# A hybrid diffusion backbone: DeltaNet on unnormalized keys and queries, with state and outputs beside the inverse

## The reference

```python
q = l2_normalize(heads(q)); k = l2_normalize(heads(k))      # x * rsqrt(sum(x*x) + 1e-6)
q = q * dk ** -0.5
kb = k * beta[..., None]
m = where(strict, (kb @ k^T) * decay, 0)
t_inv = inverse(eye + m)
u = t_inv @ (v * beta[..., None])
w = t_inv @ (kb * exp(gam)[..., None])
qk = (q @ k^T) * decay
for each chunk:                       # s is the state, carried on
    v_new = u - w @ s
    o = (q * exp(gam)[..., None]) @ s + qk @ v_new
    s = s * exp(g_last) + (k * exp(g_last - gam)[..., None])^T @ v_new
o = rms_norm(o, norm_w) * silu(z)     # norm per head over 128, eps 1e-6
```

## Time and profile before

| | |
|---|---|
| median of three executions | 2689.41 us |
| the profiled execution | 2687.36 us, span 2685.6 us, mean granted clock 0.967 |
| busy | PE 2487.0 (93%), DVE 1599.0 (60%), ACT 1000.0 (37%), POOL 80.3 (3%) |
| chain that ended last | PE 84%, DVE 9%, ACT 3%, issue 2% |
| costliest group | L1314, u products: 3 x 2208 matmuls, 811.4 + 799.8 + 799.1 us |
| 30 reciprocals of DVE, L1793 | 92.5 us, 3082 ns each |
| DeltaNet's matmuls of 64 columns, L1612 | x3952, 234.4 us |

### The profile page before, as it was taken

One profiled execution on the slowest core, in us unless ns is written; L12 is line 12 of the kernel. 1 busy time (PEld: TensorE's weight loads), 2 busy tenths in 40 slices (PEclk: granted clock), 3 DMA queues, 4 the chain that ended last, 5 costly groups with the idle time before them and its releaser, 6 DMA issues.

```text
span 2685.6 us, 37159 instructions
## 1 busy us (share of the span) xinstructions
PE 2487.0 (93%) x15516; PEld 2068.9 (77%) x15516; DVE 1599.0 (60%) x2342; ACT 1000.0 (37%) x1551; POOL 80.3 (3%) x108
## 2 busy tenths in 40 slices
PE   3999998989888999989999989999898968899999
PEld 1888876857678778868887868888685758889899
DVE  5777665367766674577655553333446676566654
ACT  2322223355653422233222232232246563344543
POOL 0000000000012100000000000000000002200000
PEclk8999999999889999999999999999999989999999
DMA  6455542101100043325554422222220210045454
GB/s 256 173 188 188 188 157 94 63 32 63 63 32 2 17 157 110 125 96 204 187 190 169 157 88 94 100 104 95 94 95 32 94 63 2 2 144 186 158 185 161
DMA packets 44661, 309.62 MB, mean 115 GB/s; under 512 B 5072, under 2 KB 6224, under 8 KB 7632
## 3 DMA queue, kind: packets, MB, share of 16 engines
q1 hardware_dynamic: 44208, 305.98, 31.6%
q10 hardware_dynamic: 288, 1.27, 0.1%
HBM read 306.18 MB, written 1.05 MB: 114 GB/s over the span
## 4 chain that ended last, share of the span: by engine, by line
PE 84%; DVE 9%; ACT 3%; issue 2%; DMA 1%; SPq 0%; ACTq 0%; DVEq 0%
PE bank L1314 69%; PE bank L1612 7%; PE bank L1307 2%; DVE rt L1793 2%; PE bank L1558 1%; PE bank L1536 1%; DVE w_lo L1782 1%; DMA ring<-in_wts 1%; DVE u_lo L1822 1%; DVE sq L1832 1%; ACT L850 1%; PE bank L1545 1%; ACT w_hi L832 1%; PE bank L1345 1%; DVE work L2184 1%
## 5 line engine op out<-in xcount | busy, mean ns | idle before, releaser
L1782 DVE TENSOR_TENSOR w_lo<-ring,w_hi 128x1024 fp32r<-128x1024 f32 x420 | 510.8, 1224 | 704.9 <-ACT w_hi L832 700.9
L1314 PE MATMUL bank<-u_hi,w_hi 128*128 128x512 f32 (+1 forms) x2208 | 811.4, 367 | 85.6 <-DVE w_lo L1782 48.6
L1314 PE MATMUL bank<-u_hi,w_lo 128*128 128x512 f32 (+1 forms) x2208 | 799.8, 362 | 0.0
L1314 PE MATMUL bank<-u_lo,w_hi 128*128 128x512 f32 (+1 forms) x2208 | 799.1, 362 | 0.0
L832 ACT ACTIVATE w_hi<-ring 128x1024 fp32r<-128x1024 f32 x420 | 443.0, 1058 | 884.0 <-PE bank L1314 882.2
L1314 PEld LDWEIGHTS bank<-u_hi,w_hi 128*128 128x128 f32 x2208 | 422.8, 191 | 166.3 <-issue 67.3
L1314 PEld LDWEIGHTS bank<-u_hi,w_lo 128*128 128x128 f32 x2208 | 423.2, 192 | 65.0 <-issue 3.1
L1314 PEld LDWEIGHTS bank<-u_lo,w_hi 128*128 128x128 f32 x2208 | 422.4, 191 | 63.6
L1612 PE MATMUL bank<-work 64*64 64x64 f32 (+1 forms) x3952 | 234.4, 247 | 37.9 <-DVE work L2187 21.4
L1612 PEld LDWEIGHTS bank<-work 64*64 64x64 f32 (+1 forms) x3952 | 221.8, 161 | 50.0 <-POOL work L806 31.8
L1314 PE MATMUL bank<-hidden_hi,w_hi 128*128 128x512 f32 (+1 forms) x704 | 258.9, 368 | 0.0
(11 more groups left out here) (207 smaller groups left out, 2512.3 us busy)
## 6 DMA issues: line engine op xcount, KB each, us to landing
ring<-in_wts SPq DMA_DIRECT2D x288, 1024.0 KB, 4.8
h<-in_x SPq DMA_DIRECT2D x8, 256.0 KB, 10.8
par<-in_par ACTq DMA_DIRECT2D x2, 620.0 KB, 6.1
out<-h SPq DMA_DIRECT2D x8, 128.0 KB, 3.5
cst<-in_cst SPq DMA_DIRECT2D x1, 704.0 KB, 10.2
mod_par<-in_mod SPq DMA_DIRECT2D x1, 96.0 KB, 9.7
cond<-in_c SPq DMA_DIRECT2D x1, 8.0 KB, 1.7
```

Of the source, the lines that this page charges most:

```text
L1314: last = weights.used(pe.matmul(out, lhs[a], rhs[b], start=start and n == 0, stop=stop and n == 2))
L1782: tt(w_lo[:, b % HALVES, :], half_source(n % RING, part), w_hi[:, b % HALVES, :].bitcast(F32), ALU.subtract).then_inc(panel_left[n % RING] ...
```

## The change

It has three parts.

1. **Norms.** Keys and queries stay as they are. The squared key norms are summed as columns (keys as the stationary side against one column of ones, 16 products into `bank[4]`), rooted once per layer into `key_norm` (128x16). Values are scaled by it when they are copied into token order; beta is divided by it twice. Outputs of DeltaNet then carry the query norm and the missing factor, which goes into the epsilon of the output norm: its sum of squares gets the squares of q times `query_eps`, and a constant `out_eps`, as columns too. The root is taken once (128x16), inverted once, and spread over partitions by products with the identity (`spread_root`). Key and value transpositions go through banks 5 and 6 behind each z product. The norm helpers of `(l, "qk")` and `(l, "o")` go.
2. **Order in DeltaNet.** Banks 0 to 3 (`FRESH`, `STATE`) are used beside 4 to 7. The product w = kg^T T and its copy go; instead k x S (`keyed`) is subtracted from the values before the inverse is applied. New values of step j - 1 are taken after the Gram products of step j, its states and outputs stand between the halves of level 1, key-query products in level 2, `keyed` in level 3, and decay exponents of step j + 1 before the corner.
3. **Start.** x is loaded first, under semaphores of its own. Square sums begin with its first four chunks; PE sums them after three adaLN panels instead of eight; the modulations come after the reciprocal; the first weight panel is split after the first chunk of u.

```diff
             sp.dma_start(cond[:, :, :], c_d).then_inc(cond_in, 16)
+            for k in range(DC):
+                sp.dma_start(h[:, k, :], x_d[k * P:(k + 1) * P, :]).then_inc(x_in[k // 4], 16)
             for i in range(RING):
                 sp.dma_start(ring[:, i * PANEL:(i + 1) * PANEL], wts[i]).then_inc(panel_in[i], 16)
...
@@ ACT, norm (DVE has the same behind its chunk 1) @@
                 for k in range(DC):
+                    if k == 1 and l == i == 0:
+                        splits.upto(START[0, "gu", 0] + 1)
...
@@ ACT, qkv and z @@
-                    if c >= 4:
-                        qk_square(c - 4)
-                    if c >= 5:
-                        root((l, "qk", c - 5), 1.0)
+                    if 5 <= c < 9:
+                        key_square(c - 5)
                     if c >= 9:
                         z_silu(c - 9)
-                        tok_copy(c - 9)
-                root((l, "qk", 7), 1.0)
+                        if c == 9:
+                            key_norms()
+                        keep_keys(c - 9)
+                        keep_values(c - 9)
                 z_silu(3)
-                for i in range(3, 8):
-                    tok_copy(i)
+                keep_keys(3)
+                keep_values(3)
...
@@ ACT, DeltaNet @@
+                def decays(j):
+                    for d in range(2):
+                        act.wait_ge(decay_masked[d], l * 4 + j + 1)
+                        act.activation(E[:, d, :], E[:, d, :], ACT.Exp).then_inc(decay_exp[d], 1)
+                        act.wait_ge(gain_ready[d], l * 4 + j)
+                        act.activation(EG[:, d, :], FRESH[d][:, :], ACT.Exp).then_inc(gain_exp[d], 1)
+                def fresh_values(d, j):
+                    act.wait_ge(fresh_made[d], l * 4 + j + 1)
+                    scaled_heads(V[:, d, :], FRESH[d], beta[:, ORDER[d][j], 4 * d:4 * d + 4]).then_inc(fresh_ready[d], 1)
...
@@ PE, start @@
-            for p in range(ADA_FIRST):
+            for p in range(RING):
                 ada(0, p)
-            pe.wait_ge(inputs_in, 16 * (DC + 2))
+            pe.wait_ge(inputs_in, 16 * 2)
+            sums((0, "norm", 0))
+            for p in range(RING, ADA_FIRST):
+                ada(0, p)
...
@@ PE, behind the first z product @@
+                    if i == 0:
+                        pe.wait_ge(keys_squared, 4 * (l + 1))
+                        for t in range(4):
+                            for hd in range(HEADS):
+                                last = pe.matmul(bank[4][:, HEADS * t + hd:HEADS * t + hd + 1], k_sq[:, hd, t * P:(t + 1) * P],
+                                                 ones[:, 0:1], start=True, stop=True)
+                        last.then_inc(keys_summed, 1)
...
@@ PE, a step of DeltaNet @@
+                    def beside_level(n, d):
+                        if n == 1 and j:
+                            outs(d, j - 1)
+                        elif n == 2:
+                            key_query(d, j)
+                        elif n == 3 and j:
+                            keyed(d, j)
+                    for d in range(2):
+                        if it:
+                            pe.wait_ge(y_kept[d], it * LEVELS)
+                        each(lambda hd, c, t: mm(TWO[d][:, c], kT[:, hd, t], kT[:, hd, t]), d, j).then_inc(kk_made[d], 1)
+                    if j:
+                        for d in range(2):
+                            fresh(d, j - 1)
+                    for n in range(1, LEVELS):
+                        for d in range(2):
+                            if n == 1 and j:
+                                state(d, j - 1)
+                            first_half(n, d)
+                        beside_level(n, 0)
+                        for d in range(2):
+                            second_half(n, d)
+                        beside_level(n, 1)
+                    if j < 3:
+                        for d in range(2):
+                            decay(d, j + 1)
...
+                pe.wait_ge(queries_squared, l + 1)
+                for i in range(HEADS):
+                    pe.wait_ge(outs_squared, HEADS * l + i + 1)
+                    for t in range(nt):
+                        total = bank[4][:, 4 * i + t:4 * i + t + 1]
+                        pe.matmul(total, q_sq[:, i, t * P:(t + 1) * P], query_eps, start=True, stop=False)
+                        last = pe.matmul(total, o_sq[:, i, t * P:(t + 1) * P], ones[:, 0:1], start=False, stop=True)
...
@@ DVE, behind the updates of level n @@
+                        if n == 1 and j:
+                            for d in range(2):
+                                add_output(d, j - 1)
+                            new_state(0, j - 1)
+                        elif n == 2:
+                            if j:
+                                new_state(1, j - 1)
+                            for d in range(2):
+                                gained_queries(d, j)
+                        elif n == 3:
+                            for d in range(2):
+                                scores(d, j)
+                        elif n == 4 and j:
+                            for d in range(2):
+                                keyed_values(d, j)
+                    if j < 3:
+                        decays(j + 1)
```

More of the change, by code:

```diff
@@ L535, in backbone @@
         cond_in = sem("cond_in")
+        x_in = [sem(f"x_in{i}") for i in range(2)]
         inputs_in = sem("inputs_in")
@@ L1429, in _ @@
                 nt = w // P
-                sums((l, "norm", 0))
+                if l:
+                    sums((l, "norm", 0))
                 ffn(l, 0, T, 0 if l == 0 else None, (3 * l) * DC)
@@ new lines, in each, with mm, by_block @@
+                def each(what, d, j):
+                    t = ORDER[d][j]
+                    for hd in range(HEADS):
+                        last = what(hd, slice(hd * P, (hd + 1) * P), slice(t * P, (t + 1) * P))
+                    return last
+                def mm(out, lhsT, rhs, start=True, stop=True):
+                    return pe.matmul(out, lhsT, rhs, start=start, stop=stop)
+                def by_block(out, lhsT, rhs):
+                    for hd in range(HEADS):
+                        for rows in (LOW, HIGH):
+                            last = mm(out[rows, hd * BLOCK:(hd + 1) * BLOCK], lhsT[rows, hd, :], rhs[rows, hd, :])
+                    return last
@@ L1602, in _ @@
+                for d in range(2):
+                    decay(d, 0)
                 for j in range(4):
                     it = l * 4 + j
-                    tiles = [ORDER[d][j] for d in range(2)]
-                    def each(what, d):
-                        for hd in range(HEADS):
-                            last = what(hd, slice(hd * P, (hd + 1) * P), slice(tiles[d] * P, (tiles[d] + 1) * P))
-                        return last
-                    def mm(out, lhsT, rhs, start=True, stop=True):
-                        return pe.matmul(out, lhsT, rhs, start=start, stop=stop)
@@ new lines, in keyed_values, with add_output @@
+                def keyed_values(d, j):
+                    dve.wait_ge(keyed_made[d], 3 * l + j)
+                    t = ORDER[d][j]
+                    for hd in range(HEADS):
+                        c = slice(hd * P, (hd + 1) * P)
+                        last = stt(V[:, d, c], STATE[d][:, c], egam[:, d, t, hd:hd + 1], vtok[:, t, c], ALU.mult, ALU.add)
+                    last.then_inc(keyed_ready[d], 1)
+                def add_output(d, j):
+                    t = ORDER[d][j]
+                    if j % 2 and t < nt:
+                        out = yb[:, :, t * P:(t + 1) * P]
+                        dve.wait_ge(out_made[d], outs_before(l, j, d) + 1)
+                        dve.wait_ge(out_kept[1 - d], outs_before(l, j, 1 - d))
+                        tt(out, out, heads(FRESH[d][:, :]), ALU.add).then_inc(out_kept[d], 1)
```

452 lines of the change are left out of this document (245 added, 207 removed).

## The result

The kernel after takes 2607.28 us (median of four, 2605.19 to 2614.93) against 2689.24 for the kernel before (median of four, 2688.88 to 2689.96): a ratio of 0.970, interval 0.968 to 0.972. The profiled execution took 2605.19 us, with a span of 2603.4 and a mean granted clock of 0.976. That is 82.2 us less than the profiled execution of before; the forecast had 91.0.

The account below looks back on a forecast made before the run. The prediction took PE, with its waits and half-clock stretches, to bound the kernel. Its terms, 12 + 24.6 + 27.9 + 19.2 + 18.1 - 10.8 = 91.0 us, gave 2598.4 from a median of 2689.4, range 2582 to 2630.

Parts of the forecast that it names:

- The start: Kernel start: PE's first wide product at 41.8, third at 57.9; gain taken as 12 us, bounds 6 and 14.
- the hole behind the adaLN products: Kernel start: PE waits for `w_lo` standing behind the next panel's adaLN products on DVE, a new 3.6 us hole.
- qkv and z: Each layer's qkv and z stage, fewer reciprocals and sums: gains 24.6 us in layer 0, 27.9 in layer 1.
- DeltaNet: DeltaNet stages with reordered chunk steps: 130.9 us in layer 0 (gain 19.2), 125.0 in layer 1 (gain 18.1).
- Rival (a): DeltaNet: interleaving gives nothing because in-order queues couple both chains; gain 8 of 37 us, 2627; chance 0.16.
- The output norm: Output norm: one-column sums and spreading products in PE's queue; loss 7.2 us in layer 0, 3.6 in layer 1.
- rival (c): DeltaNet: PE falls to 1.2 GHz on short products with small gaps; slower, up to 2840; chance 0.02.
- Rival (b): Start and z stage give back their gain through the adaLN hole and ACT's value copies; 2617; chance 0.15.
- Rival (d): DeltaNet: more than forecast, full clock also in the first step and groups at 0.94; 2586; chance 0.12.

## Why the prediction was right, step by step

**The start** was right in place and size: first product at 42.12 (41.8 forecast), third at 57.56 (57.9), the hole behind the adaLN products there. The 1 us that I took off for clock lost behind the hole was not lost (PE is at full clock from 45.6 on), so the 12 was 0.9 low; the run with the old start shows the term alone.

**qkv and z** came within 1 us in both layers: a gain of 13.2 in layer 0 and 12.8 in layer 1 up to the end of the last qkv product (12.7 forecast), then 32.0 us to DeltaNet (31.3), in layer 1 24.5 (25.1). The sum hides two errors that cancel or stay off the path: the clock fell in or right behind the one-column key sums in both layers, which I had not priced, and what DVE's reciprocals alone cost is less than the waits that went with them.
On ACT's table switches in layer 1's chain the row stands against the drain once more, the next ACTIVATE starts 1.29 us after the switch:

```profile
2118.20 1.28 ACT L1106 ACT_TABLE_LOAD   x1
2119.49 0.63 ACT L1106 ACTIVATE work<-work 128x512 f32<-128x512 f32 x1
```

By the drain of 1.38 that the Trainium skill (ScalarE: Activation LUTs, "What ACT_TABLE_LOAD costs") adds, the stage would have taken an estimated 3 us longer than the forecast; it took 0.6 less.

**DeltaNet** was right in size, 132.3 and 127.0 us for 130.9 and 125.0, with steps as forecast. PE's longest wait in each middle step is one of about 1 us, for POOL's masks and no longer for DVE's start matrices. My reasons for it were half right. Rival (a), that the interleaving gives nothing, is nearly true of the levels (5 us of 34). It is false of the other half of the reordering, new values and states under the start of the inverse: that is worth 54 us against a serial order. I had priced that cover at 5 us of waiting a step and left out that the clock falls with the pauses, 3 us of the 9. No run puts the product w back, so its share is open.

**The output norm** is the step that failed. The prediction took the full clock for granted: 32 one-column products at 6.8 us. They took 12.1 (5.3 more), and slowed the gate product by 1.6. Together 6.9 us; the term missed 6.6 in layer 0, most of the 8.8 us by which the whole forecast was too high. The row for the price had 16 records, so eight such products, at full pace; it shows no fall. The 7.2 isn't the sum of its own terms either: 6.8 + 4.2 - 0.9 - 4 x 0.85 is 6.7, and the pause of 0.9 stayed (863.18 behind 862.32), which would make it 7.6. That 13.8 less 6.9 of clock comes so near 7.2 is in part luck: the 16 spreading products took 3.5 us, not 4.2. I looked for a fallen clock in DeltaNet (rival (c)), whose short products have 64 and 128 columns and keep 1.00 from the second step on in this trace, and not in the sums. In layer 1 the 16 products fit in at full pace and the clock fell behind them, over the first gate product: 1.0 more than in the run with 128 columns, inside the 3.6. That is in part luck too: in four of the seven traces with these sums it fell within them in layer 1.

**Rival (b)**, the start and the z stage giving back, did not happen. **Rival (c)** did not either: 762:862 has a clock of 1.00. **Rival (d)** did not: the first step still has a clock of 0.89 up to 762.

## What to carry to other kernels

A matmul's price is its time at the clock that it leaves behind: a run of one-column products that looks cheapest was dearer than the same run with 128 columns. When work is moved to fill PE, look for the stretch in which PE has nothing at all (here the start of the inverse), since it pays twice, in the wait and in the clock behind it; spreading work through a stretch that is already full gave almost nothing here (3.2 us of the median). And line up the two traces by a count of products that both share: here it put most of the error on one line of the table.

## What the hardware showed unexpectedly

The granted clock fell to 0.50 while PE's record was busy without a gap: 10.00 of 10.00 us between 865 and 875. It did so in layer 0's sums with one column a product (12.1 us for 32 products, and in each of the nine traces that have one-column sums there) and with 32 columns (12.8), and not with 128 (7.1; both layers of three traces) nor, for 16 products of the keys, with 64 (both layers of one trace); at full clock all of them take 0.22 us a product. When it falls varies from trace to trace, and 16 one-column products in a row often end before it does. The Trainium skill (TensorE: Matmul & The Clock Gate, "What's actually happening") says that the clock follows how busy PE has been; the busy share of this profile does not predict it here.
